# Local attention of a two-layer transformer kernel: value tiles with high and low half side by side

## The reference

```python
def sliding_window_sink_attention(q, k, v, sinks, valid):
    kb, vb = band(k), band(v)            # the block before and the own block, 256 keys
    scores = jnp.einsum('bnqhgd,bnkhd->bnhgqk', qb, kb) * scale
    mask = ((diff >= 0) & (diff < WINDOW))[None] & kvalid[:, None, :]
    scores = jnp.where(mask[None, :, None, None], scores, -jnp.inf)
    probs = jax.nn.softmax(jnp.concatenate([scores, sink], axis=-1), axis=-1)[..., :-1]
    return jnp.einsum('bnhgqk,bnkhd->bnqhgd', probs, vb).reshape(B, L, Hq * d)

y_sw = (o_sw * jax.nn.silu(sw_z)) @ w_branch_swa[l]
merged = jax.nn.sigmoid(g_sb) * y_sb + jax.nn.sigmoid(g_sw) * y_sw
```

## Time and profile before

| | |
|---|---|
| median of 3 runs | 967.26 us (967.25 to 967.8) |
| the profiled execution, its own time | 967.46 us |
| its span, first to last instruction | 965.7 us |
| TensorE busy in the span | 951.2 us (99%) |
| VectorE | 632.4 us (65%) |
| ScalarE | 467.7 us (48%) |
| GpSimd | 272.7 us (28%) |

### The profile page before, as it was taken

The page is one execution under the profiler, slowest core; times in us unless marked ns, Lnnn a source line. Parts: engine busy times, 40 slices in busy tenths (PEclk is TensorE's granted clock), DMA queues, the critical chain, the costliest instruction groups (busy, mean ns, idle before and its releaser), DMA issues.

```text
span 965.7 us, 12818 instructions
## 1 busy us (share of the span) xinstructions
PE 951.2 (99%) x4798; PEld 801.1 (83%) x4798; DVE 632.4 (65%) x914; ACT 467.7 (48%) x852; POOL 272.7 (28%) x198
## 2 busy tenths in 40 slices
PE   7999999999999999999999999999999999999997
PEld 6988888888888888888888888988888887888886
DVE  5677787946787687864755887699547775312314
ACT  5435665725444665634447778523555652221212
POOL 2216200003226200002253010151358884314141
PEclk9999999999999999999999999999999999999999
DMA  9332201132422201133222111122220113232312
GB/s 298 102 117 74 93 23 44 44 131 84 151 88 88 88 26 61 46 130 85 88 88 88 44 45 43 45 88 88 88 87 22 45 44 107 89 103 94 131 44 87
DMA packets 64990, 80.37 MB, mean 83 GB/s; under 512 B 5520, under 2 KB 48656, under 8 KB 64928
## 3 DMA queue, kind: packets, MB, share of 16 engines
q1 hardware_dynamic: 63024, 76.64, 24.6%
q10 hardware_dynamic: 1904, 2.88, 0.9%
HBM read 77.42 MB, written 2.10 MB: 82 GB/s over the span
## 4 chain that ended last, share of the span: by engine, by line
PE 54%; issue 31%; ACT 5%; DVE 5%; POOL 4%; DMA 1%; POOLq 0%; ACTq 0%; DVEq 0%
PE ps L1977 14%; PE ps L1979 14%; PE ps L1978 14%; PE ps L2035 2%; PE ps L2036 2%; PE ps L2034 2%; PE ps L2500 1%; DVE sp L1740 1%; ACT spr L1013 1%; POOL small L588 1%; POOL small L601 1%; DMA x<-in_x 1%; DVE wlo L1646 1%; ACT qsb L1013 1%; PE ps L2509 1%
## 5 line engine op out<-in xcount | busy, mean ns | idle before, releaser
L633 POOL TENSOR_TENSOR wlo<-raw,whi 128x2048 fp32r<-128x2048 f32 (+1 forms) x23 | 101.0, 4393 | 184.9 <-ACT whi L1007 175.5
L1977 PE MATMUL ps<-whi,hhi 128*128 128x512 f32 (+1 forms) x320 | 115.8, 362 | 1.0 <-ACT sp L1105 0.3
L1979 PE MATMUL ps<-whi,hlo 128*128 128x512 f32 (+1 forms) x320 | 114.5, 358 | 0.0
L1978 PE MATMUL ps<-wlo,hhi 128*128 128x512 f32 (+1 forms) x320 | 114.4, 358 | 0.0
L1977 PE MATMUL ps<-hhi,whi 128*128 128x512 f32 x288 | 113.5, 394 | 0.6 <-POOL wlo L704 0.6
L1979 PE MATMUL ps<-hhi,wlo 128*128 128x512 f32 x288 | 112.4, 390 | 0.0
L1978 PE MATMUL ps<-hlo,whi 128*128 128x512 f32 x288 | 112.2, 390 | 0.0
L1007 ACT ACTIVATE whi<-raw 128x2048 fp32r<-128x2048 f32 (+1 forms) x29 | 53.0, 1826 | 84.4 <-PE ps L1979 75.9
L1317 DVE TENSOR_TENSOR wlo<-raw,whi 128x2048 fp32r<-128x2048 f32 (+1 forms) x29 | 63.5, 2190 | 37.4 <-ACT whi L774 30.9
L774 ACT ACTIVATE whi<-raw 128x2048 fp32r<-128x2048 f32 (+1 forms) x29 | 52.1, 1797 | 69.2 <-PE ps L1979 69.2
L2034 PE MATMUL ps<-hhi,whi 128*128 128x512 f32 x192 | 76.8, 400 | 0.0
(11 more groups left out here) (338 smaller groups left out, 2291.6 us busy)
## 6 DMA issues: line engine op xcount, KB each, us to landing
raw<-in_w_in SPq DMA_DIRECT2D x42, 1024.0 KB, 5.3
raw<-in_w_out SPq DMA_DIRECT2D x12, 1024.0 KB, 5.1
raw<-in_w_in SPq DMA_DIRECT2D x10, 512.0 KB, 4.1
raw<-in_w_branch_swa SPq DMA_DIRECT2D x4, 1024.0 KB, 5.0
raw<-in_w_branch_sb SPq DMA_DIRECT2D x4, 512.0 KB, 3.4
x<-in_x ACTq DMA_DIRECT2D x3, 512.0 KB, 6.8
out<-x SPq DMA_DIRECT2D x3, 512.0 KB, 2.6
ws<-in_spatial_w SPq DMA_DIRECT2D x2, 512.0 KB, 6.4
```

Source lines behind the costliest of these rows:

```text
L633: pool.tensor_tensor(wlo[s][:, 0:n, :], raw[s][:, 0:n, :], whi[s][:, 0:n, :].bitcast(F32), ALU.subtract).then_inc(slab_split, 1)
L1977: pe.matmul(out_ap, lhsT=lhi(k), rhs=rhi(k), start=first and k == 0, stop=False, skip_group_check=True)
L1978: pe.matmul(out_ap, lhsT=lhi(k), rhs=rlo(k), start=False, stop=False, skip_group_check=True)
L1979: m = pe.matmul(out_ap, lhsT=llo(k), rhs=rhi(k), start=False, stop=last and k == n - 1, skip_group_check=True)
```

## The change

The four value tiles become two. `step` and `before` hold the high part of each 64-wide group in columns 0 to 63 and its low part in columns 64 to 127. One matmul with such a tile gives the product with the high values in partitions 0 to 63 of bank 6 and that with the low values in partitions 64 to 127. So a turn has four value matmuls for six; a term that was left out before (low values times low probabilities) comes in with them. The halves have to be added: ScalarE copies, for even and odd heads, the other half from PSUM to a tile `other` in SBUF (two copies of 64x256), VectorE adds bank 6 and `other` (two additions of 64x256), which frees bank 6, waits for its own additions, and multiplies by the gate over all 128 partitions in one instruction, from SBUF to SBUF. The making of the value tiles has half of the instructions on ScalarE and GpSimd. `pwt` is there twice, so `transposed_hi(w)` waits for the values of w - 2. VectorE does `transposed_lo(w)` ahead of `window_out(w - 1)`, and ScalarE `window_other_half(w - 1)` behind `transposed_hi(w)`. `window_out_hi` waits for the gating.

```diff
-            for copy_ in range(2):
-                values_low(step_lo, v_step[:], step_hi, copy_).then_inc(vw_lo, 1)
+            values_low(step, v_step[:]).then_inc(vw_lo, 1)
             pool.wait_ge(vw_hi, 2)
             pool.wait_ge(tw_done, 10)
-            for copy_ in range(2):
-                values_low(before_lo[:, 0:1], insert_dim(v_meta[:], 1, 1), before_hi[:, 0:1], copy_)
-                values_low(before_lo[:, 1:], tokw[:, 0:3, 1152:1280], before_hi[:, 1:], copy_).then_inc(vw_lo, 1)
+            values_low(before[:, 0:1], insert_dim(v_meta[:], 1, 1))
+            values_low(before[:, 1:], tokw[:, 0:3, 1152:1280]).then_inc(vw_lo, 1)
...
             def window_own_low(w):
 
                 pool.wait_ge(tw_lo, 10 + w + 1)
-                pool.tensor_tensor(by_head(pwt[:, 1, 1, :]), by_head(pwt[:, 1, 0, :].bitcast(F32)),
+                p = pwt[:, w % 2, 1]
+                pool.tensor_tensor(by_head(p[:, 1, :]), by_head(p[:, 0, :].bitcast(F32)),
                                    insert_dim(own_keys.bitcast(F32), 1, 4), ALU.mult).then_inc(window_own_lo, 1)
...
             def transposed_hi(w):
                 act.wait_ge(tw_done, 10 + w + 1)
+                if w >= 2:
+                    act.wait_ge(swo_done, w - 1)
+                copy(pwt[:, w % 2, 0, 0, :], ps[:, 4 + w % 2, :]).then_inc(tw_hi, 1)
+
+            def window_other_half(w):
+
+                act.wait_ge(swo_done, w + 1)
                 if w:
-                    act.wait_ge(swo_done, w)
-                copy(pwt[:, 0, 0, :], ps[:, 4 + w % 2, :]).then_inc(tw_hi, 1)
+                    act.wait_ge(swo_read, w)
+                for e in range(2):
+                    r, o = slice(64 * e, 64 * e + 64), slice(64 - 64 * e, P - 64 * e)
+                    last = copy(other[r], ps[o, 6, :].rearrange("p (c e n) -> p c e n", c=2, e=2)[:, :, e, :])
+                last.then_inc(other_done, 1)
...
             for w in range(16):
                 transposed_hi(w)
+                if w:
+                    window_other_half(w - 1)
...
             def window_out(w):
 
                 n, u = turn_of(w)
-                dve.wait_ge(swo_done, w + 1)
+                dve.wait_ge(other_done, w + 1)
                 if w >= 2:
                     dve.wait_ge(ysw_ready, w - 1)
                 for e in range(2):
                     r = slice(64 * e, 64 * e + 64)
                     o = ps[r, 6, :].rearrange("p (c e n) -> p c e n", c=2, e=2)[:, :, e, :]
-                    last = dve.scalar_tensor_tensor(yw[r, w % 2], o, 0.5, gate_sw[r, 2 * u:2 * u + 2, n * P:n * P + P],
-                                                    ALU.mult, ALU.mult)
+                    last = dve.tensor_tensor(yw[r, w % 2], o, other[r], ALU.add)
                 last.then_inc(swo_read, 1)
+                dve.wait_ge(swo_read, w + 1)
+                dve.scalar_tensor_tensor(yw[:, w % 2], yw[:, w % 2], 0.5, gate_sw[:, 2 * u:2 * u + 2, n * P:n * P + P],
+                                         ALU.mult, ALU.mult).then_inc(window_gated, 1)
...
             for w in range(16):
+                transposed_lo(w)
                 if w:
                     window_out(w - 1)
-                transposed_lo(w)
...
-                pe.matmul(ps[:, 6, :], lhsT=v(before_hi), rhs=pwt[:, 0, 0, :], start=True, stop=False)
-                pe.matmul(ps[:, 6, :], lhsT=v(before_lo), rhs=pwt[:, 0, 0, :], start=False, stop=False)
+                pe.matmul(ps[:, 6, :], lhsT=v(before), rhs=p[:, 0, 0, :], start=True, stop=False)
                 pe.wait_ge(tw_lo, 10 + w + 1)
-                pe.matmul(ps[:, 6, :], lhsT=v(before_hi), rhs=pwt[:, 1, 0, :], start=False, stop=False)
+                pe.matmul(ps[:, 6, :], lhsT=v(before), rhs=p[:, 1, 0, :], start=False, stop=False)
                 pe.wait_ge(window_own_hi, w + 1)
-                pe.matmul(ps[:, 6, :], lhsT=v(step_hi), rhs=pwt[:, 0, 1, :], start=False, stop=False)
-                pe.matmul(ps[:, 6, :], lhsT=v(step_lo), rhs=pwt[:, 0, 1, :], start=False, stop=False)
+                pe.matmul(ps[:, 6, :], lhsT=v(step), rhs=p[:, 0, 1, :], start=False, stop=False)
                 pe.wait_ge(window_own_lo, w + 1)
-                pe.matmul(ps[:, 6, :], lhsT=v(step_hi), rhs=pwt[:, 1, 1, :], start=False, stop=True).then_inc(swo_done, 1)
+                pe.matmul(ps[:, 6, :], lhsT=v(step), rhs=p[:, 1, 1, :], start=False, stop=True).then_inc(swo_done, 1)
```

More of the change, by code:

```diff
@@ L148, in build @@
         row_gain = sb("row_gain", [P, D])
-        step_hi = sb("step_hi", [P, NT, 2, 2, HD], F32R, at[0] - 4 * KB)
+        step = sb("step", [P, NT, 2, 2, HD], F32R, at[0] - 4 * KB)
         r_gain = at[0]
@@ L226, in build @@
         gate_sw = sb("gate_sw", [P, 8, SEQ])
-        step_lo = sb("step_lo", [P, NT, 2, 2, HD], F32R)
         r_tokm = region(4 * KB)
-        before_hi = sb("before_hi", [P, NT, 2, 2, HD], F32R, r_tokm)
+        before = sb("before", [P, NT, 2, 2, HD], F32R, r_tokm)
         tokm = sb("tokm", [META, 1, 256], F32, r_tokm)
@@ L236, in build @@
         pw = sb("pw", [P, 4, 2, 130])
-        at[0] = tok_start + 5 * KB
-        before_lo = sb("before_lo", [P, NT, 2, 2, HD], F32R)
-        pwt = sb("pwt", [P, 2, 2, SEQ], F32R)
+        other = sb("other", [P, 2, P])
+        pwt = sb("pwt", [P, 2, 2, 2, SEQ], F32R)
         tz = sb("tz", [P, 2, SEQ], F32, tok_start + 20 * KB)
@@ L394, in build @@
         yb_ready = sem("yb_ready")
-        sqp_done = sem("sqp_done")
         o_scaled = sem("o_scaled")
@@ L441, in build @@
         sw_exp = sem("sw_exp")
+        other_done, window_gated = sem("other_done"), sem("window_gated")
         pw_ready = sem("pw_ready")
@@ L677, in _, with values_low @@
                         .then_inc(v_step_ready, 1)
-            def values_low(lo, v, hi, copy_):
-                return pool.tensor_tensor(lo[:, :, :, copy_, :], v.rearrange("p t (g d) -> p t g d", g=2),
-                                          hi[:, :, :, copy_, :].bitcast(F32), ALU.subtract)
+            def values_low(tile, v):
+                return pool.tensor_tensor(tile[:, :, :, 1, :], v.rearrange("p t (g d) -> p t g d", g=2),
+                                          tile[:, :, :, 0, :].bitcast(F32), ALU.subtract)
             pool.wait_ge(vw_hi, 1)
-            for copy_ in range(2):
-                values_low(step_lo, v_step[:], step_hi, copy_).then_inc(vw_lo, 1)
+            values_low(step, v_step[:]).then_inc(vw_lo, 1)
             pool.wait_ge(vw_hi, 2)
             pool.wait_ge(tw_done, 10)
-            for copy_ in range(2):
-                values_low(before_lo[:, 0:1], insert_dim(v_meta[:], 1, 1), before_hi[:, 0:1], copy_)
-                values_low(before_lo[:, 1:], tokw[:, 0:3, 1152:1280], before_hi[:, 1:], copy_).then_inc(vw_lo, 1)
+            values_low(before[:, 0:1], insert_dim(v_meta[:], 1, 1))
+            values_low(before[:, 1:], tokw[:, 0:3, 1152:1280]).then_inc(vw_lo, 1)
             def window_out_lo(w):
@@ L1141, in values_high @@
             def values_high(hi, v):
-                for copy_ in range(2):
-                    last = copy(hi[:, :, :, copy_, :], v.rearrange("p t (g d) -> p t g d", g=2))
-                return last
+                return copy(hi[:, :, :, 0, :], v.rearrange("p t (g d) -> p t g d", g=2))
             for half in range(2):
@@ L1150, in _ @@
                     act.wait_ge(v_step_ready, 2)
-                    values_high(step_hi, v_step[:]).then_inc(vw_hi, 1)
+                    values_high(step, v_step[:]).then_inc(vw_hi, 1)
                 for t in range(NT):
@@ L1181, in _ @@
             act.wait_ge(rope2_done, 5)
-            act.wait_ge(vw_lo, 2)
-            values_high(before_hi[:, 0:1], insert_dim(v_meta[:], 1, 1))
-            values_high(before_hi[:, 1:], tokw[:, 0:3, 1152:1280]).then_inc(vw_hi, 1)
+            act.wait_ge(vw_lo, 1)
+            values_high(before[:, 0:1], insert_dim(v_meta[:], 1, 1))
+            values_high(before[:, 1:], tokw[:, 0:3, 1152:1280]).then_inc(vw_hi, 1)
             def transposed_hi(w):
                 act.wait_ge(tw_done, 10 + w + 1)
-                if w:
-                    act.wait_ge(swo_done, w)
-                copy(pwt[:, 0, 0, :], ps[:, 4 + w % 2, :]).then_inc(tw_hi, 1)
+                if w >= 2:
[3 more added lines that the diff above has]
+                act.wait_ge(swo_done, w + 1)
+                if w:
+                    act.wait_ge(swo_read, w)
[3 more added lines that the diff above has]
+                last.then_inc(other_done, 1)
             def window_exp(w):
@@ L1226, in window_out_hi @@
                 n, u = turn_of(w)
-                act.wait_ge(swo_read, w + 1)
+                act.wait_ge(window_gated, w + 1)
                 copy(qw[:, 4 * u:4 * u + 4:2, n * P:n * P + P], yw[:, w % 2]).then_inc(yw_hi, 1)
@@ L1244, in _ @@
                     merge_tanh(1 + GATE_ENDS.index(w + 1))
+            window_other_half(15)
             window_out_hi(15)
@@ L1879, in transposed_lo @@
```

(18 more changed lines are left out.)

1 line of the change is left out of this document (removed).

## The result

The changed kernel takes 970.34 us (median of 7 runs, 970.06 to 971.17), the kernel before 967.55 in the same comparison (7 runs, 967.25 to 967.98): a ratio of 1.0028, 95% interval 1.0019 to 1.0037. It is 2.8 us slower, although TensorE has 32 matmuls less. The forecast was 968.1, with a range of 963.3 to 971.2.

What follows compares the result with a forecast made beforehand. TensorE bounds the kernel now; after the change VectorE's 4.72 us round would. Twelve rounds 56.6 + 0.9 + 0.4 = 57.9, 1.1 more; stage end 0.4 less: 967.46 + 0.7 = 968.2, stated as 968.1 (range 963.3 to 971.2).

Steps and rivals of the forecast that it cites:

- case C: Gating behind window_own_low needs its full 0.45 us, waiting for slab parts too: 3.0 us more, 971; chance 0.26.
- The unhindered round, 4.17 us: VectorE's round after the change without meeting GpSimd: 4.17 us, level with TensorE's new mean of 4.12.
- Line 1881 behind `window_normalised`: VectorE's two-tile SBUF product waits for GpSimd until 1.30 us after the reciprocal and ends at 1.85.
- The gating behind `window_own_low`: VectorE's gating, ready 2.66 us after the reciprocal, waits for GpSimd until 2.99; the maxima start 0.20 later.
- TensorE waits for `swo_read`: TensorE waits for VectorE's additions in most rounds, 0.3 to 1 us each, as VectorE's round is 4.72.
- The slab parts, 0.9 us: GpSimd's slab parts delay VectorE's rounds by 0.1 to 0.25 us each, 0.9 for five up to round 11.
- Slab 19's round, 0.4 us: Slab 19's last quarter ends at about 767.5; TensorE waits in round 9, VectorE's low part comes 0.4 us late.
- a lower clock: Sign of a wrong forecast: granted clock below 1.0 in the stage because TensorE now pauses.
- The end of the stage, 13.6 us: From round 12's reciprocal to the first matmul behind the stage: 13.6 us, where it was 14.0.
- ScalarE at nothing: ScalarE's two added copies from PSUM, about 0.7 us a turn, cost nothing because it has room every round.
- Rival A: No hindrance of VectorE by GpSimd: rounds 4.17 us at TensorE's pace, 6.7 us gained, 960.7; chance 0.17.
- Rival B: Only one VectorE-GpSimd meeting, the gating escapes: round about 4.45 us, 3.3 less, 964.9; chance 0.13.

Runs made afterwards that it cites:

- both_psum: Changed kernel with the gating and the product with own_keys both reading an operand from PSUM instead of SBUF; 962.41 us, ratio 0.9944.
- own_psum: Changed kernel with the product with own_keys taken from PSUM instead of pwt in SBUF; 963.25 us, ratio 0.9952.
- no_halves_slab: Changed kernel without ScalarE's copy and the additions, and with slab 19's quarters split a round earlier; 963.3 us, ratio 0.9952.
- slab_early: Changed kernel with the four quarters of slab 19 split in rounds 3, 4, 5, 6 instead of 3, 4, 6, 7; 968.55 us, ratio 1.0008.
- six_no_halves: Changed kernel without ScalarE's copy and the additions, with two of the four value matmuls issued twice; 967.17 us, ratio 0.9994.
- gate_psum: Changed kernel with the additions writing into bank 6 and the gating reading it there, in PSUM; 968.96 us, ratio 1.0007.
- no_halves: Changed kernel without ScalarE's copy of the other half and without the additions, gating from PSUM; 965.02 us, ratio 0.997.
- old_order: Changed kernel with VectorE's old order, window_out(w - 1) ahead of transposed_lo(w); 978.5 us, ratio 1.0111.

## Why the prediction was right, and where its sizes were off

The direction and the mechanism were right: the 7.4 us of matmuls don't arrive because VectorE's round grows past TensorE's, and it grows by its meetings with GpSimd. The forecast lay 2.2 us below the result, 0.3 of it because the kernel before came out at 967.55 in this comparison and not at 967.26. The result is inside the range (963.3 to 971.2) but outside the forecast's own part of it (966.3 to 969.4): it is case C by its number (slower by over 0.2%, chance 0.26), with part of C's mechanism. The round of 4.84 us is still one of the forecast's (4.6 to 4.85). Going through the steps:

- *The unhindered round, 4.17 us.* The kernel without meetings shows 4.16 (`both_psum`), but that is luck: from start to next start the reciprocal takes 0.09 there and not 0.2, the low part 0.57 and not 0.61, and the gating 0.46 (741.92 to 742.38) and not 0.34. The errors cancel.
- *Line 1881 behind `window_normalised`: n + 1.30, then 0.55.* Measured n + 1.29 and 0.55 (735.57, 736.86, 737.41). Its worth in time, from `own_psum`, is about 7 us (970.34 to 963.25), with what the slab 19 round gives back.
- *The gating behind `window_own_low`.* The meeting at n + 2.99 came at n + 2.98 (738.55). The term that was mis-sized is what follows: I took 0.20 us to the next start, from line 1881's overlap behind a wait, and it is 0.31 (738.55 to 738.86). The fault is in the 0.34: free, the gating takes 0.46 to the next start, and 0.46 less the same 0.14 is 0.32. It doesn't overlap with its successor as line 1881 does. In this round the reciprocal's error can't cancel it, since line 1881 waits for GpSimd in any case. With the maxima at 1.55 for 1.53 this is 0.12 a round and 1.4 us in twelve. Case C had the place right and its price at 0.25 for what is 0.11. The sign "the gating near 0.8" didn't fit my own layout, which gives 0.62 (2.66 to 2.99, then 0.29); measured is a mean of 0.607.
- *TensorE waits for `swo_read`.* Only in part. I expected a wait for the additions in most rounds; there are four, 1.9 us. Five others, 3.2 us, are for `window_own_low` in front of the last value matmul, which comes late behind a slab part. I had laid out that lateness and not said that TensorE waits for it.
- *The slab parts, 0.9 us.* They cost VectorE nothing: rounds with and without a part are 4.82 to 4.85. `window_out_lo` ended at 750.31, the very time at which `window_normalised` could start (0.25 behind the reciprocal of 750.06). I had it 0.1 us later. `no_halves_slab` shows where the cost would begin: GpSimd's turn with a part is 4.63. This 0.9 too much hid as much of the other misses; that the sum came as near as it did is luck to that extent.
- *Slab 19's round, 0.4 us.* It costs 1.7 (6.56 against 4.84), and 1.8 by `slab_early`. I had its end at 767.5 and it was 767.6. What I had left out is that TensorE ran at half clock behind the stop: 1.2 us up to the value matmuls, with the transposes for which VectorE waits (see the run with `own_keys` out of PSUM). With the 0.4 that is nearly all of the 1.7. I had named a lower clock as a sign that would prove me wrong; it was this case's second largest miss.
- *The end of the stage, 13.6 us.* Measured 13.5 (790.63 to 804.16).
- *ScalarE at nothing.* Two copies take 0.77 us, near the 0.7 estimated, and VectorE waits for one of them once, 1.5 us, in the last turn (until 805.16), off TensorE's path. It also waits for ScalarE's high part, 4.5 us in four waits: the longest are 2.1 us behind slab 19, where ScalarE itself waits for the transposes, and 1.4 in turn 14, where the copy of the gated product and a tanh stand ahead of it in ScalarE's queue. I had not listed the second, which lies in the end of the stage.

In sum 1.4 - 0.9 + 1.3 = 1.8 of the 2.0 us by which the forecast's 0.7 was below the measured 2.67; the rest is round 10, which starts late behind slab 19.

Rival A would have been right for the kernel with both operands in PSUM (960.7 forecast; 962.4 measured, 961.0 without the slab 19 stop). Rival B, the gating alone set free, was priced at 3.3 us and measured 1.4 by the medians (970.34 to 968.96) and 2.0 by the ratios (0.0021): its place was right and its price too high. I took 0.27 a round; my own layout gives 0.19 (3.00 for 3.19 to the next start), and measured is 0.18 (4.66 for 4.84). The making of the value tiles wasn't tried alone; in `six_no_halves` it is in, beside the second `pwt` and the new order, and the three together change nothing measurable.

## What to carry to other kernels

Taking work from the busiest engine is worth what the next longest round allows: lay out each engine's round before and after, instruction by instruction, in units of start to next start, and ask where VectorE and GpSimd will both read SBUF. Where an operand of VectorE also lies in PSUM, read it there: here that one change of operand was worth 7 us of 970, the half clock that went with it included, about as much as the 32 matmuls (7.4). In the kernel before, where VectorE doesn't hold the round, the same edit and slab 19 a round earlier were worth only 1.8 us together. And when a stage gets tighter, look at the work that has a due time of its own, like a slab split in quarters: one stop of TensorE brought a stretch at half clock with it, 1.8 us together in the changed kernel.

## What the runs showed of the hardware

- A waiting VectorE instruction went ahead of GpSimd's next one at every handover that the timelines above show, and in every other turn of the changed kernel's trace. GpSimd's next 128x512 instruction then ended 1.11 to 1.16 us behind VectorE's end, where it takes 1.28 undisturbed.
- A two-tile instruction of VectorE behind such a wait ends 0.55 us after it for 128x512 (0.68 free) and 0.29 for 128x256 (0.42 free): 0.13 less than its free time in both cases.
- In the traces the granted clock fell behind stops of 1.96 us (changed kernel), 1.95 (`gate_psum`), 1.88 (`no_halves`) and 1.48 (`old_order`), and not behind 1.37 (`own_psum`), 1.10 (`both_psum`) or 0.59 us (the kernel before). This is no threshold: each is one execution, and four of the eleven of `gate_psum` have a mean granted clock (0.999, the others 0.996 or 0.997) that speaks against such a fall. It was back at 2.4 GHz some 3 us later each time.
